# Two-layer decoder step, attention stage: probabilities and sample keys turned in 64-row halves, two tiles at a time, each pair copied by two engines

## What is computed

```python
def nsa_block(q, g, q_pos, kc, vc, kc_end, ks, vs, kw, vw, kw_pos):
    qg = q.reshape(B, Q, KV_HEADS, GROUP, HEAD_DIM) * (HEAD_DIM ** -0.5)
    s_c = jnp.einsum('bqhgd,bnhd->bhgqn', qg, kc)              # compressed keys
    p_c = masked_softmax(s_c, kc_end[None, :] <= q_pos[:, None])
    o_c = jnp.einsum('bhgqn,bnhd->bqhgd', p_c, vc)
    ...                                                        # ranking of key blocks by p_c: the 16 best
    p_s = masked_softmax(s_s, (pos_sel <= q_pos[:, None]))     # selected blocks
    o_s = jnp.einsum('bhgqn,bhqnd->bqhgd', p_s, v_sel)
    p_w = masked_softmax(s_w, (rel >= 0) & (rel < WINDOW))     # window of 512
    o_w = jnp.einsum('bhgqw,bwhd->bqhgd', p_w, vw)
    o = gq[..., 0:1] * o_c + gq[..., 1:2] * o_s + gq[..., 2:3] * o_w
    return o.reshape(B, Q, W_ATTN)
```

## Time and profile before

| | us |
|---|---|
| time, median of 3 runs | 1151.45 (1147.46 to 1152.38) |
| span of the profiled execution | 1144.9 |
| attention, first score step to the start of the output projection behind the last value step | 399.7 to 728.6 |
| PE, DVE, ACT, POOL busy in the span | 1100.2, 744.2, 381.9, 370.9 |

### The profile page before, as it was taken

One profiled execution on the slowest core, in us unless ns is written; L12 is line 12 of the kernel. 1 busy time (PEld: TensorE's weight loads), 2 busy tenths in 40 slices (PEclk: granted clock), 3 DMA queues, 4 the chain that ended last, 5 costly groups with the idle time before them and its releaser, 6 DMA issues.

```text
span 1144.9 us, 17799 instructions
## 1 busy us (share of the span) xinstructions
PE 1100.2 (96%) x7048; PEld 916.0 (80%) x7048; DVE 744.2 (65%) x1341; ACT 381.9 (33%) x812; POOL 370.9 (32%) x382
## 2 busy tenths in 40 slices
PE   6999999999999989989999999999999999999997
PEld 6888999999988945556655556787899999998875
DVE  3677889999883588846455646585754740159655
ACT  3202111222323466767556656320121212235000
POOL 3543620000001578763576365310022312208000
PEclk9999999999999989989999999999999999999999
DMA  7753512253220032140384035642131110131321
GB/s 231 242 157 132 184 38 56 56 196 108 51 60 1 3 120 74 29 157 1 110 289 155 1 139 174 142 134 79 42 112 54 37 55 20 42 147 75 110 97 60
DMA packets 85883, 113.65 MB, mean 99 GB/s; under 512 B 21952, under 2 KB 67144, under 8 KB 85727
## 3 DMA queue, kind: packets, MB, share of 16 engines
q1 hardware_dynamic: 71849, 69.51, 19.7%
q0 software_dynamic: 11776, 41.95, 10.8%
q10 hardware_dynamic: 2182, 1.16, 0.4%
HBM read 100.91 MB, written 16.64 MB: 103 GB/s over the span
## 4 chain that ended last, share of the span: by engine, by line
PE 85%; DVE 5%; issue 3%; POOL 2%; DMA 2%; ACT 2%; another core or an unknown queue 0%; SPq 0%; ACTq 0%; DVEq 0%
PE PS L697 25%; PE PS L2002 15%; PE PS L1770 14%; PE PS L1247 6%; PE PS L1261 6%; PE PS L1127 5%; PE PS L685 3%; PE PS L1794 2%; PE PS L1165 2%; DMA WRAW<-in_w_in_even 2%; PE PS L1783 1%; DVE ACC L557 1%; PE PS L1982 1%; DVE PS L1343 1%; PE PS L1223 1%
## 5 line engine op out<-in xcount | busy, mean ns | idle before, releaser
L604 DVE SCALAR_TENSOR_TENSOR Y<-U,SM,Y 128x1024 f32<-128x1024 f32 x120 | 147.9, 1296 | 0.3
L697 PE MATMUL PS<-XH,WH 128*128 128x352 f32 (+1 forms) x648 | 146.9, 331 | 0.0
L697 PE MATMUL PS<-XL,WH 128*128 128x352 f32 (+1 forms) x648 | 144.0, 326 | 0.0
L697 PE MATMUL PS<-XH,WL 128*128 128x352 f32 (+1 forms) x648 | 143.2, 325 | 0.0
L697 PEld LDWEIGHTS PS<-XH,WH 128*128 128x128 f32 (+1 forms) x648 | 107.9, 186 | 2.7
L697 PEld LDWEIGHTS PS<-XH,WL 128*128 128x128 f32 (+1 forms) x648 | 108.2, 185 | 1.4
L697 PEld LDWEIGHTS PS<-XL,WH 128*128 128x128 f32 (+1 forms) x648 | 107.9, 185 | 1.4
L2109 POOL TENSOR_TENSOR WL<-WRAW,WH 128x1024 fp32r<-128x1024 f32 x14 | 37.5, 2675 | 210.7 <-ACT WH L2054 210.7
L288 POOL TENSOR_TENSOR WL<-WRAW,WH 128x1024 fp32r<-128x1024 f32 x12 | 28.7, 2390 | 232.6 <-ACT WH L361 232.5
L557 DVE SCALAR_TENSOR_TENSOR ACC<-PS,SM,ACC 128x508 f32<-128x508 f32 x124 | 86.9, 742 | 25.2 <-PE PS L685 21.7
L1343 DVE CUSTOM_DVE_ANT_0 PS<-PS,MASKC 128x512 f32<-128x512 f32 (+7 forms) x96 | 62.4, 690 | 27.8 <-PE PS L1247 26.5
(11 more groups left out here) (335 smaller groups left out, 2113.5 us busy)
## 6 DMA issues: line engine op xcount, KB each, us to landing
WRAW<-in_w_in_even SPq DMA_DIRECT2D x16, 512.0 KB
WRAW<-in_w_in_odd SPq DMA_DIRECT2D x16, 512.0 KB, 4.0
TM<-in_state_win_kv SPq DMA_DIRECT2D x12, 512.0 KB
XIN<-in_x_prompt SPq DMA_DIRECT2D x8, 512.0 KB, 13.6
WRAW<-in_w_in_even SPq DMA_DIRECT2D x16, 256.0 KB
XR<-in_x_prompt SPq DMA_DIRECT2D x8, 512.0 KB, 3.5
layer_out<-R SPq DMA_DIRECT2D x8, 512.0 KB, 2.7
XR<-layer_out SPq DMA_DIRECT2D x8, 512.0 KB, 3.3
```

Source lines behind the costliest of these rows:

```text
L604: v.scalar_tensor_tensor(dst, src, CWT[:, i, t:t + 1], dst, ALU.mult, ALU.add).then_inc(s_cv, 1)
L697: ins = pe.matmul(PS[0:mcols, 3 * slot + c, 0:CH], w[:, slot, kk, 0:mcols], x[:, kk, c * CH:(c + 1) * CH], start=(kk == 0 and n == 0), sto ...
```

## The change

1. **Turning in 64-row halves.** A block of 128x128 is turned as two halves of 64 rows. The upper half goes to bank 4, the lower half to bank 5, each with 64 columns.
2. **Two tiles at a time.** Tiles of one group of three units are paired (`PAIRED`, 80 turnings in place of 148), so that both banks are full. ACT copies bank 4, DVE bank 5, each into its 64 columns of every block. `PT` has two buffers of two tiles.
3. **The samples' keys and probabilities** go through the same two banks (20 and 6 turnings) in place of bank 7 (40 and 12). The next turning of any sort waits for both copies of the one before (`turn_free`).
4. **The mask `M` writes SBUF** (`probs`), and the exponential works there in place. A bank of scores is thus free after `M`, and `M` waits for the last turning of the unit three before.
5. **The planner** knows durations by kind, a handover for each dependence, a price for changing PE's kind of tiling, and takes the step with the most work behind it (`remains` plus a table `PREFER`) among those that can begin within 200 ns of the first.

The diff, cut to its core:

```diff
-        PRC = at("PRC", [P, GROUP, 64], F32, 60928)
-        PT = [at(f"PT{i}", [P, 512], F32, o) for i, o in enumerate((61952, 64000, 123520))]
+        PRC = [at(f"PRC{x}", [P, 64], F32, o) for x, o in enumerate((67072, 67328, 126112, 126368))]
+        PT = [at("PT0", [P, 2, 512], F32, 60928), at("PT1", [P, 2, 14624], F32, 65024)]
...
+        def turn(kind, what, blocks, after, copied):
+            step("PE", kind, what, 62 * blocks, *after, mode=BY_ROWS)
+            step("ACT", "P", ("ACT", what), 120 + 60 * blocks, (what, PE_END), *copied)
+            step("DVE", "P", ("DVE", what), 130 + 70 * blocks, (what, PE_END), *copied)
...
+            def turn_free(x):
+                if turn_no[x]:
+                    pe.wait_ge(s_ptea, turn_no[x])
+                    pe.wait_ge(s_pted, turn_no[x])
+
+            def turn_halves(c, rows, x):
+                for a in range(2):
+                    half = slice(64 * a, 64 * a + 64)
+                    ins = pe.transpose(PS[0:rows, 4 + a, c:c + 64], x[half, :], ident[half, half])
+                return ins
...
-                    bank7_free(x)
-                    if i < 4:
-                        pe.wait_ge(s_ring[i % 2], 64 * (3 * (b // 4) + i // 2 + 1))
...
+                    turn_free(x)
+                    for j in range(2):
...
+                        for c in range(4):
+                            ins = turn_halves(256 * j + 64 * c, P, RING[:, i % 2, b % 4, c * 256:c * 256 + P] if i < 4 else window(b)[:, c, 0:P])
...
-                                pe.wait_ge(s_exp, row_waits[j] + 1)
+                                pe.wait_ge(s_nm, row_waits[j] + 1)
...
-                    if t >= 2:
-                        pe.wait_ge(*evac_count(t - 2))
-                    for h in range(2):
-                        for gl in range(2):
-                            c = 256 * h + P * gl
-                            ins = pe.transpose(PS[0:cols, 4 + t % 2, c:c + P], probs(u, 2 * gl + h, i * P, cols), ident[:, :])
+                    turn_free(ev)
+                    for j, t in enumerate(PAIRED[ev[1]]):
+                        u, i = TURNS[t]
+                        cols = NCP if UNITS[u][2] == CMPB else P
+                        for h in range(2):
+                            for gl in range(2):
+                                ins = turn_halves(256 * j + 64 * (2 * h + gl), cols, probs(u, 2 * gl + h, i * P, cols))
...
+            elif x[0] == "kt":
+                _, group, i, pair = x
+                eng.wait_ge(s_rank, 2)
+                used = kt_before(x)
+                if used:
+                    eng.wait_ge(s_xf, bank7_filled(used))
+                ins = half(KTS[pair][:, :, :].rearrange("p j (c r) -> p (j c) r", r=P), 0)
...
                 if ev[0] == "M":
                     _, p, h = ev
+                    u = p // 2
+                    if u >= 3 and h == 0:
+                        v.wait_ge(s_tpt, turn_no[("T", last_turn[u - 3])] + 1)
                     v.wait_ge(s_sc, 2 * p + h + 1)
-                    lowest(scores_of(p, h), scores_of(p, h), mask_of(p // 2), NMX[:, stat(p, h):stat(p, h) + 1]).then_inc(s_nm, 1)
+                    lowest(probs(u, 2 * (p % 2) + h, 0, nkeys(u)), scores_of(p, h), mask_of(u), NMX[:, stat(p, h):stat(p, h) + 1])\
+                        .then_inc(s_nm, 1)
```

More of the change, by code:

```diff
@@ L936, in program @@
         TURNS = [(u, i) for u in range(len(UNITS)) for i in range(len(key_tiles(u)))]
-        unit_last_turn = {u: t for t, (u, i) in enumerate(TURNS)}
-        PV_PARTS = 6
-        todo = {e: {} for e in ("PE", "DVE", "ACT", "POOL")}
-        def step(engine, kind, what, ns, *after):
-            todo[engine].setdefault(kind, []).append((what, ns, [x for x in after if x]))
+        PAIRED = []
+        for q in range(0, len(UNITS), 3):
+            ts = [t for t, (u, i) in enumerate(TURNS) if q <= u < q + 3]
+            PAIRED += [ts[k:k + 2] for k in range(0, len(ts), 2)]
@@ new lines, in program, with step @@
+        last_turn = {TURNS[t][0]: k for k, ts in enumerate(PAIRED) for t in ts}
+        PV_PARTS = 6
+        PE_END, SOON, FREED = 210, 140, 60
+        BY_ROWS, WHOLE, BY_QUARTERS, BY_HALVES = "64 rows", "128 by 128", "32 columns", "64 columns"
+        SWITCH, NEAR = 150, 200
+        SCALE_NS = {63: 430, 128: 446, 256: 670, 384: 712, 512: 945, 640: 874, 768: 978, 896: 1087, 1024: 1194}
+        todo, about = {e: {} for e in ("PE", "DVE", "ACT", "POOL")}, {}
+        def step(engine, kind, what, ns, *after, mode=None):
+            todo[engine].setdefault(kind, []).append(what)
+            about[what] = (engine, kind, ns, [x for x in after if x], mode)
@@ L982, in take @@
         def take(engine, x, ns, *after):
[L983 to L994 removed]
+            step(engine, "X", ("take", x), ns, (x, PE_END), *after)
@@ L1053, in program @@
         for tt in range(2):
-            step("PE", "Y", ("Y", tt), 5200, ("wol", 3), ("wol", 2), ("E", NP - 1, 1))
-        URGENT = {"PE": "SXTVY", "DVE": "PRMOQHXW", "ACT": "PXEW", "POOL": "CXAW"}
-        HANDOVER = 130
+            step("PE", "Y", ("Y", tt), 5540, (("wol", 3), SOON), (("wol", 2), 160), (("M", NP - 1, 1), SOON), mode=WHOLE)
+        behind = {x: [] for x in about}
+        for x, (_, _, _, after, _) in about.items():
+            for y, lag in after:
+                behind[y].append((x, lag))
@@ new lines, in program @@
+                may = []
+                for kind, line in todo[e].items():
+                    for x in line[:1] if kind != "P" else [y for y in line if y[1] == turned_last[0]]:
+                        _, _, ns, after, mode = about[x]
+                        after = list(after)
+                        if e == "PE" and kind in "TK" and turned_last[0]:
+                            after += copied(turned_last[0])
+                        if all(y in end for y, _ in after):
+                            begin = max([now[e] + (SWITCH if mode != pe_mode and e == "PE" else 0)] + [end[y] + lag for y, lag in after])
+                            may.append((begin, remains[x] + PREFER.get((e, kind), 0), kind, x))
@@ new lines, in program @@
+                if not may:
+                    continue
+                soonest = min(may)[0]
+                begin, _, kind, x = max([m for m in may if m[0] <= soonest + NEAR], key=lambda m: m[1] - m[0])
+                if first is None or soonest < first[0]:
+                    first = (soonest, begin, e, kind, x)
+            _, begin, e, kind, x = first
+            now[e] = end[x] = begin + about[x][2]
+            order[e].append(x)
+            todo[e][kind].remove(x)
+            if e == "PE":
+                pe_mode = about[x][4]
+                if kind in "TK":
+                    turned_last[0] = x
```

340 lines of the change are left out of this document (181 added, 159 removed).

## The result

| | us | against the kernel before |
|---|---|---|
| before, same chip | 1150.9 (1147.5 to 1152.4) | |
| changed kernel | 1159.8 (1157.8 to 1164.5) | 1.0083 [1.0065, 1.0101] |
| predicted | 1117 (1097 to 1150) | 0.970 |

A forecast was written before the change was run, and what follows sets the result against it. PE was taken to bound attention: its work falls from 294.0 to 242.7 us, and at 90% filled from 433 the stage ends at 696. The join comes 34 us earlier: 1144.9 - 34 = 1111, plus 6.6, 1117 us; range 1097 to 1150.

The forecast's parts named there:

- last value step: End of the attention stage: near 694 us, 696 with 2 us for the clock, in place of 728.6.
- first prompt turning: Attention's start on PE: not before about 433 us, because the window keys' copy waits for both rankings on DVE.
- from there, no gathers: Attention from 433 us on: 234.7 us of PE's work at 90% filled, 261 us, plus 2 for the clock.
- the 90%: Share of time PE's work fills in attention from 433 us; the old program filled 91% from 432.
- Half turnings: Transposes on PE: 0.061 us per pair of halves in place of 0.11 per whole tile, saving 39 us over 796.
- changes of kind: PE's tiling switches in attention: 0.15 us each, 0.21 into 64 rows; 196 runs in place of 318, 18 us less.
- Rival 3: Half turnings on PE aren't cheap: 0.107 us a pair gives 1158 us, 0.122 if loads run in turn 1171; chance 0.08.
- those 32 us: DVE's work at attention's start, from 400.2 us: queries, masks, sample steps and two rankings before the first prompt turning.
- Rival 2: Turn, copy, turn through the same two banks, with DVE's masks in the way: 82% filled, 25 us more, 1142; chance 0.15.
- The clock: PE's granted clock in attention: 2 us added, for PE leaving the longer first wait at the lower level.
- the 6.6 us from span to time: Whole kernel: the runs' median was 6.6 us above the profiled span, added to 1111 to give 1117.

The follow-up runs named there:

- after_nogather2: The changed kernel with ten of its twelve groups of indirect gathers left out, on chip 4: 1130.6 us, 0.9831 of the kernel before.
- after_third: The changed kernel, unchanged, run again as the control on chip 4: 1159.7 us, 1.0073 of the kernel before.
- win_wait: The changed kernel with the planner told when the samples' window keys land, so their turning moves later on PE: 0.9947 of the kernel before, chip 5.
- after_fourth: The changed kernel, unchanged, run again as the control on chip 6, which has no late signals: 1138.9 us, 1.0043 of the kernel before.

## Why the prediction was wrong, step by step

The forecast had the last value step end at 696; it ended at 741.4. The 45 us, by steps (from several traces, so that they add up to 44):

| step | forecast | measured |
|---|---|---|
| first prompt turning | 433 | 442.1 (434.9 once its transfer is counted) |
| from there, no gathers | 261 + 2 | 267.1 (after_nogather2: 444.1 to 711.2) |
| the gathers on top | inside the 90% | 31 (after_third, 742.3 against 711.2), 20 of them with the late signals (721.9 on chip 6) |

- **Prices and own work: right.** Half turnings at 0.061 us a pair, changes of kind at 0.15, 41 of 49 us for whole blocks. Rival 3 is out. The Trainium skill's rule ("TensorE: Matmul & The Clock Gate", LDWEIGHTS) that a load lasts by its columns holds for one load: 0.139 us for 64 rows as for 128. That the sum would double doesn't follow, since sixteen such loads pass in 0.49 us.
- **The start: 9 us too early.** I read from the order what DVE had ahead of it and forgot to ask when the first piece in front of PE could run. DVE began those 32 us late because PE held back the scores: it idled 11.7 us until 414.0. The piece was in my own list ("turned as the second piece on PE") and the earlier trace rows gave its release by the ranking; its transfer I never looked up. win_wait shows the rest of the step right to 2 us (434.9), and the transfer worth 11 us in the end.
- **90% filled: the step that failed.** I took the old order's 91% as a property of the work. It belongs to the old order, with its own banks and buffers. Without gathers the new stage from its first turning is filled to 234.7 / 267 = 88%, near the 90. With them, to 234.7 / 298 = 79%. That the first figure is near 90 is partly luck. The old kernel without gathers is filled, from 432 to the stage's end at 718.4, to 271 / 286 = 95% (an estimate with the forecast's own sum for what is done by 432), so the new order is 7 points thinner even where nothing is gathered, some 19 us. What part of that the two banks, the planner's order and the mask's new wait each have, no run here separates. The old kernel loses 15 us to the gathers, the new one 29. Of these 14 us more, 3 to 6 go with the late signals, by the chips with and without them; the rest comes with the transfers, and 6 of it can be seen as the window keys' wait on chip 6. Rival 2 had the mechanism (turn, copy, turn, 82% filled, 1142) at 15%, with DVE's masks as its cause, and missed the price: the handover I took as 0.15 us is 1.4 inside the gathers (median, on a chip with late signals).
- **The clock: too small.** I added 2 us. The granted clock over the stage is 0.92 in place of 0.97, 0.66 before the first turning and 0.95 after it, and 0.99 after it in the run without gathers. Before the first turning the missing pulses lie mostly under PE's waits. Behind it they lie mostly under its work: the 13 us by which the same matmuls take longer with gathers are of the size of the pulses missing there (4% of 298 us, 12 us). They come with the waits and are inside the 31 us above, not on top.
- **The range.** It ended at 1150, 8 us above rival 2. The start (9 us) and the gathers (31 us) both went the bad way. And the 6.6 us from span to time weren't an overhead: every later run takes 1.6 to 1.9 us more than its span, so the traced execution of before was itself some 5 us faster than the median. That moved the forecast 5 us towards the measured time.
- **The comparison.** Own work fell by 51 us. Without gathers the time fell by 5.5 (chip 4), so some 45 us went to the start and the thinner packing: by the same sums, 27 to the start (44 us with 8 of work in them, against 32 with 23) and 18 to the packing. 14 us more went to the larger toll of the gathers. The changed kernel is left 0.3 to 0.5% faster than the old one where nothing is gathered, and 0.4 to 1.0% slower where something is.

## What to carry to other kernels

Before a fill is carried over to a new order, ask what work the engine had to go on with while a handover was late. Here one pair of banks stood in front of every turning, and the same gathers cost 29 us where they had cost 15. An in-order queue waits for its first piece, so a moved piece needs its transfer's landing time looked up, and not only the engines'. When a change cuts 51 us of work and nothing comes out, leave out one neighbour at a time (here the gathers) in both kernels; the difference of the two differences is that neighbour's part, and here it was 14 us.

## What was not expected of the hardware

- While POOL issues indirect transfers (0.94 us each, 1.25 apart, four to eight in a row), signals from PE reach ACT and DVE (and POOL, in the row above) 1.4 us late in the median and up to 3.6, on three of six chips; on those without, the changed kernel's copies come within 0.15 us (after_fourth). With plain transfers of the same size from SP's queue it didn't occur. The semaphore's change is itself recorded late, and the engines begin within 0.12 us of it, so it is the signal that is held. What holds it, and what the chips differ in, is open.
- For the old kernel the gathers cost 15 us on a chip with late signals and nothing on one without: 1136.1 without gathers on a chip of 1151.0, and 1133.4 on one of 1133.3.
- A 64-row load for a transpose takes as long as a 128-row one (0.139 us), but the two of a pair begin 0.01 us apart, and pairs follow each other in 0.061 us, where whole loads take 0.11.
